# Where the spare expert blocks that carry rows stand in the expert sequence: the last spare places instead of places spread over it

## What is computed

```python
scores = jax.nn.sigmoid(jnp.dot(t, w_r).astype(F32))
biased = scores + b_r.astype(F32)
...                                  # 4 of 8 groups, then
_, idx = lax.top_k(masked, TOP_K)    # 8 of 64 experts for each of 264 tokens
w = jnp.take_along_axis(scores, idx, axis=-1)
...
def expert(acc, p):
    e_g, e_u, e_d, g = p
    a = jax.nn.silu(t @ e_g) * (t @ e_u)
    return acc + g[:, None] * (a @ e_d).astype(F32), None
routed, _ = lax.scan(expert, jnp.zeros(t.shape, F32), (wg, wu, wd, gates.T))
```

## Time and profile before

| | |
|---|---|
| median of 3 runs | 1795.79 us (1793.62 to 1798.0) |
| profiled execution | 1778.79 us |
| its span, first to last instruction | 1777.1 us |
| TensorE busy | 1629.6 us, 92% of the span |
| VectorE, GpSimd busy | 957.6 us (54%), 697.3 us (39%) |
| mean granted TensorE clock | 0.957 of full speed |
| moved by the DMA engines | 588.84 MB, mean 331 GB/s |
| expert loop of layer 0, layer 1 | starts at 273.87 and 1141.52 us |

### The profile page before, as it was taken

How to read it: one execution, slowest core, us unless ns; L and a number is a source line. 1 busy time by engine, 2 the same in 40 slices (tenths; PEclk the granted TensorE clock), 3 DMA queues, 4 the chain that set the end, 5 groups by cost and what they waited for, 6 DMA issues and landing times.

```text
span 1777.1 us, 27285 instructions
## 1 busy us (share of the span) xinstructions
PE 1629.6 (92%) x10621; PEld 914.1 (51%) x10621; DVE 957.6 (54%) x2368; ACT 238.9 (13%) x607; POOL 697.3 (39%) x755
## 2 busy tenths in 40 slices
PE   7898999999899999999779989999998999899984
PEld 4674775444445444444367557644444444444433
DVE  3887468544345544444379754764443444354436
ACT  3223331000002100000031343100000000000001
POOL 1306007554445554444102240365554455355420
PEclk9998999999999999999979979999999999999996
DMA  9668467999999999999965866599999999999955
GB/s 326 226 237 289 154 266 277 400 364 357 401 408 400 385 413 393 377 382 360 346 239 190 287 216 235 189 395 412 410 389 409 346 387 405 367 386 399 413 209 207
DMA packets 185918, 588.84 MB, mean 331 GB/s; under 512 B 67705, under 2 KB 85837, under 8 KB 131902
## 3 DMA queue, kind: packets, MB, share of 16 engines
q1 hardware_dynamic: 115504, 506.99, 73.1%
q0 software_dynamic: 67232, 79.73, 13.0%
q10 hardware_dynamic: 3054, 0.38, 0.2%
HBM read 775.22 MB, written 56.95 MB: 468 GB/s over the span
## 4 chain that ended last, share of the span: by engine, by line
PE 80%; DVE 8%; DMA 5%; issue 3%; ACT 1%; ACTq 1%; SPq 0%; POOL 0%; DVEq 0%; POOLq 0%
PE ps L1420 39%; PE ps L1433 18%; PE ps L1122 4%; PE ps L953 4%; PE ps L1268 3%; DMA raw<-in_exp_w_up,idx_w 3%; PE ps L1009 2%; PE ps L1380 1%; DMA ypart<-yrows_k 1%; DVE ysum L2277 1%; PE ps L986 1%; PE ps L1017 1%; ACTq L577 1%; PE ps L1200 1%; PE ps L1253 1%
## 5 line engine op out<-in xcount | busy, mean ns | idle before, releaser
L1420 PE MATMUL ps<-raw,xTs 128*64 128x256 f32 x6144 | 744.0, 393 | 10.3 <-DMA raw<-in_exp_w_up,idx_w 7.0
L1420 PEld LDWEIGHTS ps<-raw,xTs 128*64 128x64 f32 x6144 | 417.2, 135 | 270.5 <-issue 11.7
L1433 PE MATMUL ps<-dn,scratch 128*64 128x512 f32 x1536 | 373.1, 607 | 38.9 <-issue 37.2
L900 POOL DMA_INDIRECT yrows_k<-ytok,idx_y x192 | 196.6, 1024 | 483.9 <-DVE ytok L2104 442.0
L2209 DVE STREAM_TRANSPOSE xTs<-xg 64x256 f32<-64x256 f32 x768 | 335.6, 437 | 8.8 <-DMA xg<-hrows,idx_x 1.0
L2104 DVE COPY ytok<-ps 128x512 f32<-128x512 f32 x192 | 132.8, 692 | 280.7 <-PE ps L1433 245.8
L893 POOL DMA_INDIRECT xg<-hrows,idx_x x192 | 199.1, 1037 | 105.9 <-DVE idx_x L2193 47.8
L2098 DVE TENSOR_TENSOR scratch<-scratch,ps 128x128 f32<-128x128 f32 x192 | 55.3, 288 | 316.2 <-ACT scratch L1718 316.0
L1433 PEld LDWEIGHTS ps<-dn,scratch 128*64 128x64 f32 x1536 | 109.3, 137 | 193.2 <-issue 163.6
L1718 ACT ACTIVATE scratch<-ps 128x128 f32<-128x128 f32 x192 | 53.2, 277 | 1108.7 <-PE ps L1420 1108.7
L1122 PE MATMUL ps<-hT,wide 128*128 128x264 f32 x512 | 121.6, 394 | 6.1 <-ACT hT L1539 6.1
(11 more groups left out here) (382 smaller groups left out, 1315.9 us busy)
## 6 DMA issues: line engine op xcount, KB each, us to landing
raw<-in_exp_w_gate SPq DMA_DIRECT2D x128, 1024.0 KB, 9.9
raw<-in_exp_w_up SPq DMA_DIRECT2D x128, 1024.0 KB, 14.9
dn<-in_exp_w_down SPq DMA_DIRECT2D x128, 1024.0 KB, 13.7
narrow<-in_w_ada SPq DMA_DIRECT2D x18, 1024.0 KB, 8.8
wide<-in_w_in SPq DMA_DIRECT2D x16, 1024.0 KB, 7.7
wide<-in_w_ada SPq DMA_DIRECT2D x16, 1024.0 KB, 8.9
ypart<-yrows_k SPq DMA_DIRECT2D x16, 1024.0 KB, 13.3
raw<-in_w_ada SPq DMA_DIRECT2D x14, 1024.0 KB, 12.7
```

The source lines that it names most:

```text
L900: pool.indirect_dma_start(yrows_k.rearrange("t (h d) -> (t h) d", h=2), bass.IndirectOffsetOnAxis(ap=idx_y[:, b:b + 1], axis=0), ytok[n % ...
L1420: ins = mm(ps[64 * h:64 * h + 64, 2 + n % 2, 0:256], xTs[n % 2][:, k, :, :].rearrange("p u i -> p (u i)"), w[:, k, h], start=k == 0, stop= ...
L1433: ins = mm(ps[64 * h:64 * h + 64, 5 + n % 2, :], actT[:, n % 2, 64 * j:64 * j + 64], dn[n % NDOWN][:, j, 512 * h:512 * h + 512], start=j = ...
```

## The change

The order in which the 32 values of o are put on the 32 spare places. After it o = 0 stands at the last place (step 95), o = 1 at step 92, o = 2 at step 89, and so on, down to o = 31 at step 2. The list of steps is derived from it, and with it the block number that each step's gather, scatter and indirect weight loads use. The positions of own blocks, the number of steps and all waits stay.

```diff
 SPARE = T * TOPK // (B + 1)
 BLOCKS = NE + SPARE
 assert NE // 2 == SPARE == 32
-SPARE_AT = [(int(f"{s:05b}"[::-1], 2) + 4) % SPARE for s in range(SPARE)]
+SPARE_AT = [SPARE - 1 - o for o in range(SPARE)]
 STEPS = [b for e in range(NE) for b in ([e, NE + SPARE_AT.index(e // 2)] if e % 2 == 1 else [e])]
```

## The result

The changed kernel took 1805.74 us (median of 19 runs, 1802.13 to 1809.31) beside 1793.13 for the kernel before (19 runs, 1789.97 to 1803.27): a ratio of 1.0061, 95% interval 1.0049 to 1.0073. It is slower by 0.6%; the forecast was 1776, range 1757 to 1803, faster. The order of the instructions on each engine is the same in both kernels, and the bytes are too. The profiled execution took 1809.3 us, its span 1806.9.

The account below looks back on a forecast made before the run. It took the two expert loops on TensorE, and whatever stretches a step, as the bound. Saving 52.8 and paying 17 and 16 gave -19.8 us, 1759.0 from 1778.8, scaled by 0.96% to 1776; range 1757 to 1803.

Parts of the forecast that it names:

- The middle, 52.8 saved: Both expert loops before step 85: waits removed there save 25.5 us in layer 0 and 27.3 in layer 1.
- carriers: Spare blocks that carry rows, 3 in layer 0 and 4 in layer 1; each moves 3 x 1,048,576 bytes, 7.5 us of transfer.
- The end of layer 1, +17 (9 to 29.7): Layer 1 from step 85: three more carriers cost 17 us; floor 9 after idle transfer, ceiling 29.7 if each waits 9.9.
- The end of layer 0, +16 (12 to 25): Behind layer 0's experts: three carriers push the row read-back behind the next layer's modulation weights, costing 16 us.
- TensorE's own delay: End of layer 0: 5 to 20 us, taken to lie beside the late read-back and not added.
- The sum and the scale: Whole kernel: -52.8 + 17 + 16 = -19.8 us from 1778.8 gives 1759.0, scaled by 0.96% to 1776.
- Lag without carriers: Rival, chance 0.12: steady load keeps q0 late mid-loop at 0.37 us per step; about 1808 us, slower.
- a sign of being wrong: Middle of the loops: gathers landing 20 us after issue with no carrier would show the prediction wrong.
- Turns at the ends: Rival, chance 0.12: DMA engines alternate packets between queues, 8.9 us late per carrier, 62 for seven; about 1805, slower.
- Ends at the floor: Rival, chance 0.16: both ends cost only 26 us and a clean middle saves 58; -32 us, about 1764.
- Only the order changes: Rival, chance 0.11: transfers are saturated and bytes conserved, so only a few us of idle return; about 1793, same.

Follow-up runs that it names:

- experiment 5: Changed kernel and kernel before, unedited, rerun on one chip: 1805.53 and 1793.07; also o = 0 to 3 at steps 2, 5, 8, 11: 1793.14, without rowless spare loads 1754.29.
- experiment 1: Kernel before and changed kernel, both unedited, run again for a second trace: 1792.2 and 1799.7 us.
- first trace: Profiled execution of the unedited kernel before, on which the prediction rests: 1778.8 us, span 1777.1, no late starts; its timed median was 1795.8.
- layer 0 alone: New spare order in layer 0 only, layer 1 as in the kernel before: 1774.93 us, ratio to before 0.9977; repeated on another chip 0.9975.
- layer 1 alone: New spare order in layer 1 only, layer 0 as in the kernel before: 1772.86 us, ratio to before 0.9965.
- group N: Three chips (or occasions) on which the unedited kernel before took 1779.52, 1779.95 and 1779.62 us and no trace shows a late start.
- group L: Two chips (or occasions) on which the unedited kernel before took 1790.41 and 1793.07 us, with late starts in both kernels.
- runs without empty loads: Either order without the weight loads of spare blocks that carry no rows: 1768.26 us (0.988 of before) in the changed order, 1770.55 (0.9892) in the old.
- experiment 6: Changed kernel unedited beside before at 1779.95: 1768.09 us (0.9933); with spare up loads issued one step later 1772.99, the same edit in before 1785.8.

## Why the prediction was wrong, step by step

The account of each trace, as loss against 5.75 us a step, worked out from the starts of TensorE's steps as in the prediction. The fourth and last columns are no losses: they are the whole time from the start of step 95 to the next layer's step 0, and from there to the end in layer 1. The rows of L (5) are experiment 5's chip, those of L (1) experiment 1's.

| kernel, group | L0, 0-85 | L0, 85-95 | L0, behind | L1, 0-85 | L1, 85-95 | L1, behind |
|---|---|---|---|---|---|---|
| before, first trace (as N) | 38.5 | 1.7 | 281.2 | 29.4 | 0.0 | 60.0 |
| changed, N | 9.0 | 15.5 | 290.2 | 7.9 | 23.1 | 59.7 |
| layer 0 alone, N | 9.1 | 13.9 | 289.4 | 26.3 | 1.2 | 58.8 |
| layer 1 alone, N | 34.8 | 1.7 | 280.9 | 7.8 | 20.4 | 61.4 |
| before, L (5) | 42.0 | 1.1 | 281.5 | 36.0 | 1.0 | 60.2 |
| changed, L (5) | 34.7 | 7.4 | 292.9 | 29.9 | 12.0 | 59.2 |
| before, L (1) | 44.4 | 2.1 | 278.7 | 35.8 | 4.8 | 59.1 |
| changed, L (1) | 31.9 | 5.2 | 297.4 | 26.5 | 12.3 | 58.7 |

The numbers for L below are those of L (5), unless said otherwise.

**The middle, 52.8 saved.** On group N it is 29.5 + 21.5 = 51.0 against the first trace. No trace of the whole kernel before was taken there. By the two half changes, which are on one chip and have the old order in one layer each, it is 25.7 + 18.5 = 44.2. The reading of the carriers as the cause was right there, and its size nearly so. On group L it is 7.3 + 6.1 = 13.4 on one chip and 12.5 + 9.3 = 21.8 on the other, and this is the first step that failed. The 52.8 took for granted that nothing else stretches a step. On L each late start stretches its step by 1.0 us: 34.7 - 9.0 and 29.9 - 7.9, so 48 us in all for the changed order. The old order pays only 3.5 + 6.6 = 10 us for them (its losses on L less those of the first trace), because it had waits in the same stretch that the longer steps make unnecessary. The losses before step 85 show it when they are split by step. Steps 3k + 1, which have the late starts, lose 53.4 us in before and 55.9 in the changed kernel: both orders pay for them. All other steps lose 24.6 and 8.7, where they lose 59.0 in the first trace and 14.9 in the changed kernel on N. What the change can take away has shrunk from 44 to 16 us. The bytes asked for per us fall when the steps get longer: between 1400 and 1500 us the engines move 391 GB/s in the first trace of before and 371 in the changed kernel on L, and what is spare repays a carrier. In the trace of before on L (5) the first carrier of either layer is free and so are those at 62 of layer 0 and at 38 and 86 of layer 1, and one step of each layer stands out, 35 with 5.6 us and 63 with 5.8. On L (1) the layers have two and one such steps. The two rows that follow are the steps 85 of before on L (5).

```profile
804.98 3.84 PE L1420 MATMUL ps<-raw,xTs 128*64 128x256 f32 x32
...
1669.71 3.84 PE L1420 MATMUL ps<-raw,xTs 128*64 128x256 f32 x32
```

That two causes of waiting in one stretch don't add is also what the runs without empty loads bear out, on the chip of L (1): with the late starts nearly gone the changed order's middle is 34.8 us better than the old one's (14.0 + 4.9 for 33.3 + 20.4), where it is 21.8 better with them. The old order's losses in other steps than 3k + 1 rise from 32.4 to 47.1 us there, though loads were taken away. The ends of the changed order cost 34 us in the same two runs (13.0 + 9.5 in layer 0, 11.5 in layer 1), which is why the two orders still come out nearly alike there. That it is the bytes per us that let them go is argued, not tested.

**The end of layer 1, +17 (9 to 29.7).** The middle of the two bounds is 19, not 17. Measured 23.1 on N, 11.0 on L (7.5 on L (1), which is below the floor). TensorE's waits at the end of layer 1, changed kernel on N:

```profile
1641.13 6.14 PE L1420 MATMUL ps<-raw,xTs 128*64 128x256 f32 x32 [3.98 <-DMA raw<-in_exp_w_up,idx_w]
...
1655.06 2.48 PE L1433 MATMUL ps<-dn,scratch 128*64 128x512 f32 x8 [2.03 <-issue]
...
1666.59 5.42 PE L1420 MATMUL ps<-raw,xTs 128*64 128x256 f32 x32 [2.05 <-DMA raw<-in_exp_w_up,idx_w]
...
1680.92 3.26 PE L1433 MATMUL ps<-dn,scratch 128*64 128x512 f32 x8 [3.16 <-issue]
...
1693.12 5.45 PE L1420 MATMUL ps<-raw,xTs 128*64 128x256 f32 x32 [2.93 <-DMA raw<-in_exp_w_up,idx_w]
```

The waits sum to 14.2 of the 23.1 us; most of the rest are the slower products behind them. The windows of that kernel (busy times, granted clock, DMA share, GB/s), first the whole end, then around the first of these products:

```profile
1631.00:1712.00 81.00, 66.86 (x415) 33.71 (x413) 28.58 (x71) 2.77 (x10) 20.93 (x21) 0.87 0.90 365
...
1641.00:1647.30 6.30, 6.17 (x34) 3.92 (x36) 2.55 (x6) 0.00 (x0) 2.03 (x2) 0.60 1.02 419
```

Behind a wait of 3.98 us the mean granted clock is 0.60, so most of the 6.3 us are at the lower of the two levels, 1.2 and 2.4 GHz, and the product takes 6.14 us for 3.84. A few us of waiting are paid a second time by the clock, as in the earlier trace rows. On L the window over these steps, 1674 to 1743 us, is at a clock of 0.98 and a DMA share of 1.01. The cost there is half as large, probably because the longer steps ahead of it let the carriers' loads go out with less behind them in the queues; no run tests that. The queues in that window of the changed kernel on L, and below them those of the changed kernel on N between 1400 and 1500 us, where no carrier is near:

```profile
q1 hardware_dynamic: 2341, 17.01, 59.2%
q0 software_dynamic: 2479, 11.66, 41.5%
...
q1 hardware_dynamic: 4926, 35.90, 90.2%
q0 software_dynamic: 5303, 2.84, 9.8%
```

Counts within 6% of each other, bytes not: the same as in the earlier trace rows. But the counts are as close without any carrier, 4926 and 5303 here and 4896 and 5146 in the earlier trace rows. So they can be what each queue was given, and are no sign of turns; the prediction read too much from them. By the Trainium skill ("DMA: Bandwidth & Descriptors", section "Queues, rings and completion order") a DMA engine drains a packet of one queue and turns to the next that has work. No run here shows whether it does. The rival of turns, 8.9 per carrier and 62 at the ends, is too dear: the seven carriers cost 45.9 us on N, 6.6 each, and 28.7 on L, 4.1 each (29.3 and 4.2 on L (1)).

**The end of layer 0, +16 (12 to 25).** Measured 13.8 in the loop + 9.0 behind it = 22.8 on N, 6.3 + 11.4 = 17.7 on L. The sum counted the late row read-back at 16 and put TensorE's own delay at nothing, as lying beside it. It doesn't: they add. The read-back part is 9.0 on N, and TensorE's own delay is 13.8. VectorE's wait for the first of those reads, changed kernel on N, against 9.89 in the earlier trace rows:

```profile
873.42 0.76 DVE L2274 TENSOR_SCALAR ysum<-ypart,gk 128x1024 f32<-128x1024 f32 x1 [19.58 <-DMA ypart<-yrows_k]
```

**The sum and the scale.** On N the terms give -51.0 + 22.8 + 23.1 = -5.1, and the spans of the two profiled executions differ by 1771.7 - 1777.1 = -5.4 (the medians in experiment 6, over 28 runs of before, by -11.9). The forecast of -19.8 had the sign and the middle, and the ends 13 us too cheap. On L they give -13.4 + 17.7 + 11.0 = +15.3, for 1802.5 - 1788.4 = +14.1 between the spans and +12.5 between the medians. The remaining step that failed is the scaling. The median shown was 1% above the profiled execution; I took that for a factor on everything. It was the sign of a different kind of execution. The two traces of before on L, with their late starts, have spans of 1790.5 and 1788.4 us, 13 and 11 over the first trace, and the middle of their loops loses 12 and 10 us more. That is the same stretch as the waits that the change removes.

**The rivals.** "Lag without carriers" named the right place and sign, at 1808, but not the cause. Its symptom, which the prediction named as a sign of being wrong, is there: in the changed kernel on N gathers land 19.7 us after issue between 1400 and 1500, with no carrier since the layer began.

```profile
xg<-hrows,idx_x POOLq DMA_INDIRECT x18, 19.7
```

Yet layer 1 loses only 7.9 us before step 85 in that trace, where the rival wanted 0.37 us a step. A queue q0 that is 20 us late is nearly free while the loads are issued this far ahead. "Turns at the ends" turns the answer from 7.5 per carrier on; measured were 6.6 and 4.1. "Ends at the floor" (26 for both ends) was near on L, at 28.7, and far on N, at 45.9; the clean middle that belongs to it was seen on N alone. "Only the order changes" does not hold on either group: the differences of the spans are +14 and -5, and both timings are clear of no change.

Still open: what makes ScalarE start 2 us late on some chips, the signal or the product itself; whether it is the chip or the occasion; and whether a gap in GpSimd's run of issues would end it there.

## What to carry to other kernels

Compare the profiled execution's time with the timed runs before pricing anything by it. Where they are 1% apart, as here, the trace can be of another mode of the program, and the difference can lie just where the change acts; it is no factor to scale by. Two causes that stretch the same steps need not add: removing one gains only what the other leaves, and beside late starts of 2 us a gain of 51 us was 13 on one chip and 22 on another. And loads moved into a loop's last steps can be paid twice, by TensorE in the loop and by what is queued behind them, as in layer 0 here.

## What the runs showed of the hardware that was not expected

- On two chips of five ScalarE and SyncE start 2.0 us behind a finished product in 46 to 53 steps of an execution, while GpSimd issues seven indirect transfers in an unbroken run; on the other three the same run of issues leaves it at 0.05 us. The kernel before is 11 to 14 us slower on the first two.
- An indirect load of which every row is past the bound moves nothing and is not free: leaving out the three loads of 27 spare blocks a layer gains 20 us in the old order and 31 in the changed one on a chip with late starts, where nearly all late starts go with them. The gate and up loads alone are some 0.7% on those without.
- A wait of 4 us on TensorE cost another 2.3 us in the product behind it, at a mean granted clock of 0.60.
